# Start of a decoder layer: loads in order of first use, c spread by TensorE, eight first halves in two sweeps

## The reference

```python
mod = silu(c) @ w_mod + b_mod                      # c: 2048 values; w_mod: 2048 x 12288
sh1, sc1, g1, sh2, sc2, g2 = split(mod, 6)
h   = rms_norm(x, norm1_g) * (1 + sc1) + sh1
z   = h @ w_in                                     # 256 x 2048 by 2048 x about 5300
mix = concat(fox_attention, nsa_attention, conformer_conv)(z)
x   = x + g1 * (mix @ w_out)
h   = rms_norm(x, norm2_g) * (1 + sc2) + sh2
x   = x + g2 * (relu(h @ w_mlp1) ** 2 @ w_mlp2)
return rms_norm(x, final_g)
```

## Time and profile before

| what | value |
|---|---|
| median of 3 runs | 1237.93 us (1237.3 to 1240.41) |
| the profiled execution, its own time | 1245.03 us |
| its span, first to last instruction | 1243.3 us |
| mean granted TensorE clock | 0.972 |
| TensorE busy | 1159.6 us (93%) |
| VectorE busy | 901.8 us (73%) |
| ScalarE busy | 601.6 us (48%) |
| DMA | 307.17 MB, mean 247 GB/s |

### The profile page before, as it was taken

The page is one execution under the profiler, slowest core; times in us unless marked ns, Lnnn a source line. Parts: engine busy times, 40 slices in busy tenths (PEclk is TensorE's granted clock), DMA queues, the critical chain, the costliest instruction groups (busy, mean ns, idle before and its releaser), DMA issues.

```text
span 1243.3 us, 17218 instructions
## 1 busy us (share of the span) xinstructions
PE 1159.6 (93%) x6775; PEld 1014.3 (82%) x6775; DVE 901.8 (73%) x1009; ACT 601.6 (48%) x864; POOL 8.6 (1%) x24
## 2 busy tenths in 40 slices
PE   1789999898899998799999999999999999999995
PEld 1689998887788777799978888888888888888784
DVE  5788788999997897888776576554666646667674
ACT  5553545876655454544433344434444443444442
POOL 2000000000000000000000000000000000000000
PEclk9889999999998999799999999999999999999998
DMA  9999999456774676696576565556665556655441
GB/s 366 417 353 354 351 366 378 162 192 232 281 245 167 247 277 277 253 390 255 193 272 261 216 234 206 200 190 223 237 232 198 186 188 248 232 227 174 164 170 67
DMA packets 45912, 307.17 MB, mean 247 GB/s; under 512 B 6348, under 2 KB 7960, under 8 KB 9240
## 3 DMA queue, kind: packets, MB, share of 16 engines
q1 hardware_dynamic: 42768, 303.50, 65.4%
q10 hardware_dynamic: 3016, 2.78, 0.8%
q0 software_dynamic: 64, 0.02, 0.0%
HBM read 304.16 MB, written 2.12 MB: 246 GB/s over the span
## 4 chain that ended last, share of the span: by engine, by line
PE 69%; DVE 15%; DMA 6%; issue 5%; ACT 4%; SPq 0%; ACTq 0%; DVEq 0%
PE quad L952 14%; PE quad L965 11%; PE quad L967 11%; PE quad L966 11%; PE quad L954 7%; DMA mod_raw<-in_w_mod 4%; PE quad L942 4%; DVE w_lo L1339 4%; PE quad L944 3%; PE quad L943 3%; DVE mod_raw L1346 3%; DVE conv_y L1435 2%; ACT w_hi L669 1%; DVE acc L1357 1%; DMA raw<-in_w_mod 1%
## 5 line engine op out<-in xcount | busy, mean ns | idle before, releaser
L1339 DVE TENSOR_TENSOR w_lo<-raw,w_hi 128x1024 fp32r<-128x1024 f32 (+1 forms) x376 | 451.2, 1208 | 278.2 <-ACT w_hi L669 277.7
L669 ACT ACTIVATE w_hi<-raw 128x1024 fp32r<-128x1024 f32 (+1 forms) x376 | 391.6, 1046 | 444.5 <-PE quad L967 216.3
L952 PE MATMUL quad<-act,w_hi 128*128 128x512 f32 x768 | 271.5, 399 | 0.0
L942 PE MATMUL quad<-act,w_hi 128*128 128x256 f32 x768 | 226.2, 295 | 18.4 <-DVE w_lo L1339 13.0
L943 PE MATMUL quad<-act,w_hi 128*128 128x256 f32 x768 | 223.1, 290 | 0.0
L944 PE MATMUL quad<-act,w_lo 128*128 128x256 f32 x768 | 223.0, 290 | 0.0
L954 PE MATMUL quad<-act,w_lo 128*128 128x256 f32 x768 | 215.7, 281 | 0.0
L965 PE MATMUL quad<-w_hi,u_hi 128*128 128x512 f32 x512 | 199.8, 390 | 0.7 <-DVE u_lo L1760 0.7
L966 PE MATMUL quad<-w_lo,u_hi 128*128 128x512 f32 x512 | 199.2, 389 | 0.0
L967 PE MATMUL quad<-w_hi,u_lo 128*128 128x512 f32 x512 | 199.2, 389 | 0.0
L952 PEld LDWEIGHTS quad<-act,w_hi 128*128 128x128 f32 x768 | 144.3, 188 | 36.0
(11 more groups left out here) (265 smaller groups left out, 1103.2 us busy)
## 6 DMA issues: line engine op xcount, KB each, us to landing
raw<-in_w_main SPq DMA_DIRECT2D x184, 1024.0 KB, 4.8
mod_raw<-in_w_mod SPq DMA_DIRECT2D x78, 1024.0 KB, 6.6
late_raw<-in_w_mod SPq DMA_DIRECT2D x10, 1024.0 KB, 7.4
raw<-in_w_mod SPq DMA_DIRECT2D x8, 1024.0 KB, 9.6
x_a<-in_x SPq DMA_DIRECT2D x2, 1024.0 KB, 6.7
x<-in_x SPq DMA_DIRECT2D x2, 1024.0 KB, 8.0
out<-raw SPq DMA_DIRECT2D x4, 512.0 KB, 4.0
bias_t<-bias_scratch ACTq DMA_DIRECT2D x1, 1536.0 KB, 15.5
```

Source lines behind the costliest of these rows:

```text
L669: A(w_hi[j % 4][:, 0:2 * width], block_half(raw, j, width), ACT.Copy).then_inc(hi_done, 1)
L942: mm(out, hi, act_hi[:, k, :], start=begin and m % 2 == 0, stop=False, skip_group_check=True)
L952: mm(out, w_hi[j % 4][:, cols], act_both[:, k, :, :].rearrange("p h t -> p (h t)"), start=begin, stop=False, skip_group_check=True)
L1339: TTn(w_lo[j % 4][:, 0:2 * width], block_half(raw, j, width), w_hi[j % 4][:, 0:2 * width].bitcast(f32), ALU.subtract).then_inc(lo_done, 1)
```

## The change

1. SyncE issues the loads in order of first use: c (by partition), x, norm gain and bias, w_mod 0 to 3, two weight chunks, w_mod 4 to 6, and after a wait w_mod 7, two weight chunks, then eight small loads that ScalarE issued before. Each of the eight w_mod chunks has a place of its own (seven buffers, the third used twice), so `raw` is free for weights from the start.
2. The spread c is no longer loaded. TensorE multiplies each column of silu(c), broadcast as a 128 x 128 operand, with the identity (16 matmuls) into PSUM; ScalarE copies the rows to `acc[0]`.
3. x is scaled in two halves of its columns, and transposed in two parts: groups 0 to 3 before half 0, groups 4 to 7 at slot 2. h of pair 0 needs only w_mod 0 to 3.
4. The first eight halves go over CA, CG, FV, FE twice: k-tiles 0 and 1 of each, then 2 and 3 (half n is group n % 4, its half n // 4). Chunks 0 to 3 are laid out so on the host.
5. UNITS is reordered by k-tile: FA, FB, FC, TL are closed after their second quarter, CA, CG, FV, FE go through quarters 1, 2, 3 together, then FA, FB, FC in two quarters, NQ, NS, NC in three, TL in two. TAP_HALF moves with it from 60 to 56.
6. MODS_AT works chunks 8 to 38 in turns 5 to 59, two in turns 9, 21, 27 and 33 (before: turns 1 to 59, two in turns 7 and 17). H_AT moves.

```diff
+UNITS += [(g, 1, 1, OPEN_LONG[g], False, True) for g in OPEN_LONG]
+UNITS += [(g, q, 1, OPEN_LATE[g], q == 1, q == 3) for q in (1, 2, 3) for g in OPEN_LATE]
+UNITS += [(g, 2, 2, i, True, True) for g, i in ((FA, 0), (FB, 1), (FC, 0))]
 UNITS += [(g, 1, 3, i, True, True) for g, i in ((NQ, 1), (NS, 0), (NC, 1))]
-UNITS += [(TL, 3, 1, 0, True, True)]
+UNITS += [(TL, 2, 2, 0, True, True)]
...
+FIRST_GROUPS = 4
+HALF_AT[0:8] = [(n % 4, n // 4) for n in range(8)]
+UNIT_END = [5 + u if u < 4 else FIRST_HALF[u + 1] for u in range(N_UNITS)]
...
-MODS_AT = {2 * q + 1: 1 + (q in (3, 8)) for q in range(30) if q != 14}
+MODS_AT = {turn: 1 + (turn in (9, 21, 27, 33)) for turn in range(5, 60, 2) if turn != 45}
...
-H_AT = {10: 2, 16: 3, 23: 4, 30: 5, 38: 6, 46: 7}
+H_AT = {12: 2, 18: 3, 24: 4, 30: 5, 36: 6, 44: 7}
...
+        first_raw = [mod_raw[0], mod_raw[1], at("first_raw2", 28 * K, [P, D]), at("first_raw3", 36 * K, [P, D])]
+        first_raw += [in_hold(f"first_raw{i}", 8 * K * (i - 3), [P, D]) for i in (4, 5, 6)]
+        first_raw += [first_raw[2]]
...
-            sp.dma_start(acc[0][:, :], crow_d.to_broadcast([P, D])).then_inc(c_in, 16)
...
+            for m in range(4):
+                first_modulation(m)
+            sp.dma_start(rel_t[:, :], rel_d).then_inc(rel_in, 16)
+            sp.dma_start(onehot[:, :], onehot_d).then_inc(rel_in, 16)
+            first_block(0)
+            first_block(1)
+            for m in range(4, 7):
+                first_modulation(m)
+            sp.wait_ge(mod_step, 4)
+            first_modulation(7)
+            first_block(2)
+            first_block(3)
...
 # ScalarE
+            scale_x(0)
+            copy_x(0)
+            copy_x(1)
+            weight_hi_in(0)
+            scale_shift(0)
+            weight_hi_in(1)
+            weight_hi_in(2)
+            copy_x(2)
+            copy_x(3)
+            scale_x(1)
+            weight_hi_in(3)
+            for b in range(4, KT // 2):
+                copy_x(b)
+            bias_rows()
...
 # TensorE
+            for k in range(KT):
+                one = mm(quad[0][:, k * P:(k + 1) * P], c_act[:, k:k + 1].to_broadcast([P, P]), ident[:, :],
+                         start=True, stop=True)
...
 # VectorE
+            first_modulation(0)
+            first_modulation(1)
+            inverse_rms(0)
+            first_modulation(2)
+            first_modulation(3)
+            dve.wait_ge(col_in, 2 * 16)
+            scale_shift(0, 2, 4, n1, 0)
+            weight_lo_in(0)
+            split_h(0)
+            weight_lo_in(1)
+            weight_lo_in(2)
+            first_modulation(4)
+            weight_lo_in(3)
+            for m in range(5, MOD_FIRST):
+                first_modulation(m)
+            scale_shift(2, 2, MOD_FIRST, n1, 2)
```

More of the change, by code:

```diff
@@ L342, in build @@
         c_in = sem("c_in")
+        col_in = sem("col_in")
+        rel_in = sem("rel_in")
+        c_ps = sem("c_ps")
+        c_row = sem("c_row")
+        first_in = [sem(f"first_in{i}") for i in range(MOD_FIRST)]
         small_in = sem("small_in")
-        x_in = sem("x_in")
+        x_in = [sem(f"x_in{i}") for i in range(TT)]
         consts = sem("consts")
@@ L521, in next_quarter @@
                     sp.dma_start(raw[r % 4][:, :], main_d[r, :, :]).then_inc(raw_full[r % 4], 16)
[L523 to L526, removed]
+            for n in range(2):
+                modulation(MOD_FIRST + n, n)
             m = MOD_FIRST + 2
@@ L645, in _, with first_squares, scale_x, copy_x @@
             sqrt_table(0)
[L647 to L652, removed]
+            def first_squares(tt):
+                act.wait_ge(x_in[tt], 16)
+                for cg in range(4):
+                    n = 4 * tt + cg
+                    A(sq_a[:, n * GW // 2:(n + 1) * GW // 2].bitcast(mybir.dt.bfloat16),
+                      x_a[:, tt, cg * GW:(cg + 1) * GW], ACT.Square, accum_out=ssq[:, 0, tt, cg:cg + 1])\
+                        .then_inc(act_sq, 1)
+            first_squares(0)
+            for n in range(2):
+                act.wait_ge(c_ps, n + 1)
+                cols = slice(n * (D // 2), (n + 1) * (D // 2))
+                A(acc[0][:, cols], quad[0][:, cols], ACT.Copy).then_inc(c_row, 1)
+            first_squares(1)
             act.wait_ge(dve_ms, 1)
             A(root[:, :], mean_sq[:, :], ACT.Sqrt).then_inc(act_root, 1)
[L655 to L659, removed]
+            def scale_x(half):
+                act.wait_ge(rstd_ok, 1)
+                cols = slice(half * (D // 2), (half + 1) * (D // 2))
+                for tt in range(TT):
+                    A(x_a[:, tt, cols], x_a[:, tt, cols], ACT.Copy, scale=rstd[:, tt:tt + 1]).then_inc(xn_ok, 1)
+            def copy_x(b):
                 act.wait_ge(xt_ps, b + 1)
@@ L1019, in rows, with x_transposes @@
                 last.then_inc(pe_mod, 1)
-            pe.wait_ge(consts, 1)
-            pe.wait_ge(xn_ok, TT)
-            for b in range(KT // 2):
+            pe.wait_ge(pool_c, 2)
+            pe.wait_ge(mod_step, 1)
+            for k in range(KT):
+                one = mm(quad[0][:, k * P:(k + 1) * P], c_act[:, k:k + 1].to_broadcast([P, P]), ident[:, :],
+                         start=True, stop=True)
+                if k % (KT // 2) == KT // 2 - 1:
+                    one.then_inc(c_ps, 1)
+            def x_transposes(b):
+                pe.wait_ge(xn_ok, TT if b < KT // 4 else 2 * TT)
                 if b >= 2:
@@ L1032, in _ @@
                 last.then_inc(xt_ps, 1)
+            pe.wait_ge(consts, 1)
+            pe.wait_ge(c_row, 2)
+            for b in range(KT // 4):
+                x_transposes(b)
             def half_out(n):
@@ L1179, in _ @@
                 if slot == 2:
[L1181 removed]
+                    for b in range(KT // 4, KT // 2):
+                        x_transposes(b)
+                    pe.wait_ge(rel_in, 2 * 16)
                     mm(spare[0:NNSA, 0:S], rel_t[:, :], onehot[:, :], start=True, stop=True).then_inc(bias_ps, 1)
[L1183 removed]
                     pe.wait_ge(xt_ok, KT // 2)
[L1185 removed]
+                if slot == 3:
                     pe.wait_ge(bias_row, 1)
```

99 lines of the change are left out of this document (43 added, 56 removed).

## The result

In six timed runs each, the changed kernel took 1247.01 us (1243.87 to 1250.93) and the kernel before 1237.76 (1237.18 to 1241.31): ratio 1.0071, 95% interval 1.0057 to 1.0084. It is 0.7% slower. I had forecast 1235, with 1224 to 1244 as the range and 0.20 for slower. The measurement lies outside the range, on the side that rival 2 stood for.

The account below looks back on a forecast made before the run. TensorE, 93% busy, was taken as the bound, with VectorE bounding from the convolution to turn 91. Gains of 1.2 + 1.5, about 3 us, took 1245.03 to 1242, scaled by 0.57% to 1235 us; range 1224 to 1244.

Parts of the forecast that it names:

- rival 2: H turns directly behind chunks cost more; half 44 at 182 to 185, 3 to 6 us slower, 1242; chance 0.22.
- The start: Up to half 8: half 0 starts at 24.8 instead of 37.87, half 8 at 54.1 against 67.87.
- The stops: TensorE stands before halves 10, 22, 28, 30 and 36: 3.6, 4.7, 2.2, 5.6 and 2.2 us.
- The landing time: A w_mod chunk takes 7.5 us from issue to landing; rows showed 5.3 to 8.3, the skill page's estimate was 4.4.
- Rival 1: Chunks land sooner than 7.5 us, most lead survives; half 44 at 167 to 172, 7 to 12 gained, 1229; chance 0.32.
- the ring: Chunks 8 to 31 share two buffers, each issued only when the one two before is done; this eats the lead.
- Half 44: Start of half 44: about 179 by the hand sum, bounds about 162 to 182, taken as 176.
- So the w_mod chain ends where it did: In the projection, chunk 31 ends at 173, against 170.6 before, despite the earlier start.
- The second part: Half 44 to turn 91: convolution starts at 203.2 against 209.88; VectorE ends at 341.3 against 342.46, about 3 us gained overall.
- VectorE passes the difference on: Behind 345 us nothing differs, so the gain of about 3 us was to reach the end.
- The term of -1.5: At the conv sums TensorE is spared up to 2 us as the 2.20 stop at conv_y disappears; 1.5 taken.
- From the sum to the median: Whole kernel: 1245.03 - 3 = 1242 in the profiled execution, which was 0.57% above the median, so 1235 us.

Follow-up runs that it names:

- small_late: third_h with the eight small loads (n2, b_f, conv constants, pos) issued at SyncE's turn 46 instead of in front of chunk 8: 1222.61 us, ratio 0.9867.
- third_h: The changed kernel with a third buffer for w_mod chunks 8 to 31 and later H_AT turns: 1224.4 us, ratio 0.9874.
- third: The changed kernel with only a third buffer added for w_mod chunks 8 to 31: 1233.46 us, ratio 0.9952.
- order_only: The kernel before with only the change's list UNITS (and the TAP_HALF that follows from it): 1237.51 us, ratio 0.9996.
- cmp_first: The kernel before with the four compression weight loads issued ahead of the bias_t load in ScalarE's queue: 1245.13 us, ratio 1.0044.
- before_again: The kernel before, unchanged, timed and profiled a second time: 1238.99 us, ratio 1.0003.
- after_again: The changed kernel, unchanged, timed and profiled a second time: 1246.65 us, ratio 1.0065 against the kernel before.
- old_units: The changed kernel with the list UNITS of the kernel before beyond its first 11 units: 1248.95 us, ratio 1.0069.
- small_cmp: small_late with the compression weight loads issued ahead of bias_t, as in cmp_first: 1229.34 us, ratio 0.992.

## Why the prediction was wrong, step by step

- **What bounds the kernel.** Right: in the first part chunks, H turns and the halves behind them.
- **The start.** Predicted half 0 at 24.8, half 8 at 54.1; measured 26.54 and 54.00. Right in the main: the first chunk was worked at 12.05 instead of 10.6, which is most of what makes half 0 late, and at half 8 the lead is as predicted.
- **The stops.** Predicted before halves 10, 22, 28, 30 and 36: 3.6, 4.7, 2.2, 5.6, 2.2 us. Measured 6.1, 4.6, 0.8, 6.1, 3.5. The one that was mis-sized is half 10's: I let chunk 11 land at 59.7, and VectorE started it at 62.08 straight from the wait. SyncE's timeline shows one reason, the loads that I gave no time (start, duration of the issue):

```profile
22.74 0.67 SPq L538 DMA_DIRECT2D convw<-in_conv_w  x1
23.46 2.15 SPq L538 DMA_DIRECT2D convb<-in_conv_b  x1
25.64 2.14 SPq L538 DMA_DIRECT2D lng<-in_conv_ln_g  x1
27.83 2.14 SPq L538 DMA_DIRECT2D lnb<-in_conv_ln_b  x1
30.01 5.37 SPq L538 DMA_DIRECT2D pos_t<-in_pos  x2
35.42 1.08 SPq L498 DMA_DIRECT2D mod_raw<-in_w_mod  x2
...
51.70 0.33 SPq L498 DMA_DIRECT2D mod_raw<-in_w_mod  x1
```

The six loads in these rows before 35.42 stand in front of chunk 8's issue for 12.7 us (22.74 to 35.42). When small_late took all eight away from third_h, half 10 moved by 1.2 us, so they explain about that much of the 2.5 us. The number of buffers matters more: with the third one alone (third) chunk 11 was worked at 59.34 instead of 62.08, and the stop before half 10 was 2.90 us instead of 6.14.

- **The landing time.** I took 7.5 us for a chunk; the median over the whole program is 6.5, and with weights ahead it was more: chunk 11, issued at 51.70, landed 10.4 later. The waits behind chunk 11 came to 10.1 us (25.7 in all, less 9.1 for the very first, 0.96, 2.94 and 2.63) against 12.3. About right. Rival 1, in which the chunks land sooner, is dead. The Trainium skill (DMA: Bandwidth & Descriptors, Anatomy of one DMA) gives, for DMAs on GpSimd's path, a fixed cost of about 2.0 us and bytes at 436 GB/s. The 4.4 us for a chunk are an estimate worked out from that, and SyncE issues these chunks. For a load that has the queue to itself the traces come near it: 4.8 us for the first MB of x in the changed kernel, 4.2 for the spread c in before. For the chunks of the ring they don't: none of the 80 took less than 4.7, and between 40 and 60 us, where chunk 11 took 10.4, the DMA share is 1.00 to 1.01, so that a chunk waits for the loads in front of it.
- **Half 44.** The hand sum gave chunk 31's end at 173 and half 44 at 179. Measured: 171.08 + 2.21 = 173.3, and 178.50. Then I wrote "I take 176", a pull toward a kinder middle that no row asked for. The hand sum was right, and 178.5 lies 0.5 us from the 179 at which I had said that rival 2 decides. But by my own scale, a microsecond of time for one of half 44, 178.5 would still have been 0.5 us faster than before. So neither the ring nor rival 2 as I had priced it gives the 9 us; the error lies in the steps below.
- **"So the w_mod chain ends where it did."** This step failed. It set 173 against 170.6 of one execution. In the second profile of before, half 44 starts 4.1 us sooner, and the waits for chunks are 3.9 us instead of 10.5. The first execution had long waits for its chunks. The changed kernel repeats to 0.1 us; I take it that its waits are always long because each chunk is asked for as late as can be, but nothing that I ran tests that.
- **The second part.** Start of the convolution: predicted 203.2, measured 206.28. End of turn 91 on VectorE: predicted 341.3, measured 341.92. That they are this close is luck: the start was 3.1 us late, and VectorE's stretch 2.5 shorter than the 138.1 that I had (135.6, of which 130.0 busy, as predicted, but only 5.6 idle instead of 8.5). And "VectorE passes the difference on" was false. I subtracted 1.5 us because the stop at conv_y disappears; it did, and the stop before mix_f with its stretch at 0.51 of the clock took its place. With that stop TensorE no longer waits for VectorE at the conv sums but comes 3.8 us behind it. The conv sums start at 345.70, not near 340.0. The term of -1.5 came out at +3.5: 3.0 late at the conv sums, while VectorE is 0.5 early (341.92 against 342.45 in before). The order_only run shows this exchange without the rest of the change. This is the second step that failed.
- **From the sum to the median.** I forecast 1242 in the profiled execution's own time, and it came to 1243.87. That is luck, too: the changed kernel was 5.7 us late at the conv sums and won 4.2 back where equal code varies. Scaling by 0.57% was the third failure. The excess of before's execution was not a share of everything; 4 us of it lay in the very stage that I compared. Against the second profile the conv sums are 345.70 - 338.72 = 7.0 us late, and against cmp_first, the same code up to half 87, 345.70 - 336.96 = 8.7. That is most or all of the 9.2 between the medians here and of the 7.7 between those of before_again and after_again. Against the second profile the 7.0 are 0.35 at the start of the convolution (206.28 against 205.93), 3.1 that VectorE takes longer from there (135.6 against 132.6), and 3.5 by which the conv sums come later behind VectorE (3.8 us against 0.2). The last two are the price of the order: order_only pays them too, and old_units doesn't (132.6 and 0.2). In order_only the convolution starts early enough, at 197.52, to pay for them. In the changed kernel, for all its lead at the start, it begins at 206.28; with the ring freed, in third_h, at 184.60.

Shown by experiments: the third buffer and the H turns each take back what they were said to cost or more, TensorE's waits go with them, and the order alone, without the rest, makes no kernel slower by more than the 3 us of the intervals. Only argued, from three executions: that before's first profile was the unusual one in this stage. The same code, up to half 87, has its conv sums at 342.68, 338.72 and 336.96 (cmp_first).

Not settled: what is left of the loss, between nothing and about 2 us by which profile of before one takes; no profile shows a usual execution of the changed kernel from the conv sums to u_hi, whose timed runs have the lower clocks. Nor is it shown where cmp_first loses.

## What to carry to other kernels

A lead at the start is worth only what the next ring of buffers lets through: count how many loads may be under way at once, and where each consumer stands behind its producer in program order. Where a queue issued in one order shows a DMA share of 0.8 while its readers wait, look at what its issuer waits for; here one more buffer was the cure. Before a difference of 0.3% is forecast from one profile, take a second one of the kernel before, and compare the clocks of the profiled executions with those of the timed ones; and when a hand sum is worked out to the end, let it stand.

## What the runs showed of the hardware

- **Small loads in a long queue.** SyncE's issue of a small load took 0.43 us at 21.79 and 22.27, and 2.14 to 2.15 from 23.46 on, while the loads took 11 to 17 us from issue to landing (rows above; pos_t 5.37 for two). The two chunks behind them took 1.08 together. It isn't the shape of the loads: the same three took 0.43 us each in small_late at 155.56, where they landed after about 4 us, and 0.46 to 0.51 from ScalarE in before. Nor is it the DMA share, which was 0.99 to 1.02 in both places. What in the queue makes it long is not shown.
- **The granted clock differs between executions of one kernel.** The same window of the changed kernel, first profile:

```profile
380.00:400.00 20.00, 18.69 (x113) 15.52 (x112) 18.69 (x40) 13.11 (x29) 0.00 (x0) 0.91 0.49 176
```

and second:

```profile
380.00:400.00 20.00, 18.69 (x100) 16.13 (x98) 15.59 (x27) 11.09 (x21) 0.00 (x0) 0.74 0.44 158
```

Up to there they run together (382.15 and 381.93), with the same stop of 1.3 us for v_cmp; at u_hi they are 3.2 us apart. Why the clock differs behind the same stop is not shown.
- **The same stretch at two lengths, and at two clocks.** From the key compression to the first score with it, eight profiles took 21.6 us (21.56 to 21.59), and six took 26.1 to 27.4. TensorE stands still for the same 1.3 us inside it in both kinds. What differs is the granted clock: 1.00 in all eight, 0.71 to 0.75 in all six. Here are the first and the second profile of before:

```profile
358.11:379.70 21.59, 20.28 (x156) 17.26 (x156) 18.82 (x45) 14.05 (x30) 0.00 (x0) 1.00 0.52 195
...
356.70:383.19 26.49, 25.18 (x155) 21.50 (x155) 16.07 (x43) 11.29 (x26) 0.00 (x0) 0.74 0.36 130
```

Five of the six had waited for in_w_cmp_v just before (0.63 to 3.63 us), and small_cmp for late scores (1.48 and 0.33). Of the eight none had waited for in_w_cmp_v. But cmp_first waited 1.09 and 0.33 us for its scores and kept 1.00, so a stop doesn't always bring the lower clock. It makes about 5 us between executions, more than half of what this study was about.
